# First block of a two-block transformer kernel: products in halves of the inner dimension, keys as whole fp32 products

## The reference, cut to what matters

```python
def adaln(cond, mod_w, mod_b):
    m = jax.nn.silu(cond) @ mod_w + mod_b
    return jnp.split(m, 6, axis=-1)

def modulate(x, gain, shift, scale):
    return rms_norm(x, gain) * (1 + scale) + shift

sh1, sc1, g1, sh2, sc2, g2 = [m[:, None, :] for m in adaln(c, mod_w[i], mod_b[i])]
a = modulate(h_lat, norm1_g[i], sh1, sc1)
csh1, csc1, cg1, csh2, csc2, cg2 = adaln(c_ctx, mod_w[i], mod_b[i])
ac = modulate(h_ctx, norm1_g[i], csh1, csc1)
q, k, v, p = jnp.split(h @ w_in, [ATTN_WIDTH, ATTN_WIDTH + KV_WIDTH, ATTN_WIDTH + 2 * KV_WIDTH], axis=-1)
kc, vc = jnp.split(hc @ w_in[:, ATTN_WIDTH:ATTN_WIDTH + 2 * KV_WIDTH], [KV_WIDTH], axis=-1)
```

## Time and profile before

| | |
|---|---|
| median of 3 runs | 1664.64 us (1664.16 to 1666.16) |
| profiled execution, its own time | 1665.83 us |
| its span | 1664.1 us |
| TensorE busy | 1549.9 us, 93% of the span |
| VectorE, ScalarE, GpSimd busy | 809.1, 731.3, 572.5 us |
| DMA | 327.22 MB, 197 GB/s on average |

### The profile page before, as it was taken

How to read it: one execution, slowest core, us unless ns; L and a number is a source line. 1 busy time by engine, 2 the same in 40 slices (tenths; PEclk the granted TensorE clock), 3 DMA queues, 4 the chain that set the end, 5 groups by cost and what they waited for, 6 DMA issues and landing times.

```text
span 1664.1 us, 23167 instructions
## 1 busy us (share of the span) xinstructions
PE 1549.9 (93%) x9558; PEld 1244.8 (75%) x9558; DVE 809.1 (49%) x1430; ACT 731.3 (44%) x1049; POOL 572.5 (34%) x219
## 2 busy tenths in 40 slices
PE   5999989999998999989899999999999898899997
PEld 4867867875997778568576658999886676589996
DVE  2733578423866764154744463522437633645222
ACT  3334376423436654142455344444433454354442
POOL 1300034320000442223565125655535542256543
PEclk9999889999997899999989999999999899999999
DMA  9598269769725686753344244555543333355550
GB/s 383 203 323 286 88 266 342 263 232 387 276 94 203 250 325 235 273 204 114 127 142 134 92 182 163 177 193 177 171 138 130 126 108 135 123 204 192 193 187 26
DMA packets 51225, 327.22 MB, mean 197 GB/s; under 512 B 5936, under 2 KB 5936, under 8 KB 17456
## 3 DMA queue, kind: packets, MB, share of 16 engines
q1 hardware_dynamic: 51120, 325.73, 54.6%
HBM read 324.66 MB, written 1.05 MB: 196 GB/s over the span
## 4 chain that ended last, share of the span: by engine, by line
PE 79%; DVE 13%; ACT 3%; DMA 2%; issue 1%; POOL 1%; DVEq 0%; SPq 0%; ACTq 0%
PE ps L224 20%; PE ps L225 19%; PE ps L226 19%; PE ps L221 17%; DVE lo L232 4%; DMA raw<-in_wmod 2%; PE ps L2712 1%; DVE s L240 1%; DVE pb L2763 1%; DVE s L232 1%; POOL lo L232 1%; ACT hi L229 1%; DVE pb L232 1%; DVE gl L232 1%; DVE s L2467 1%
## 5 line engine op out<-in xcount | busy, mean ns | idle before, releaser
L232 POOL TENSOR_TENSOR lo<-raw,hi 128x2048 fp32r<-128x2048 f32 (+2 forms) x76 | 350.2, 4618 | 648.1 <-ACT hi L229 648.1
L229 ACT ACTIVATE hi<-raw 128x2048 fp32r<-128x2048 f32 (+2 forms) x192 | 350.5, 1858 | 43.9 <-POOL big L232 16.9
L232 DVE TENSOR_TENSOR lo<-raw,hi 128x2048 fp32r<-128x2048 f32 (+1 forms) x116 | 298.1, 2586 | 96.4 <-ACT hi L229 96.4
L232 POOL TENSOR_TENSOR loh<-rawh,hih 128x1024 fp32r<-128x1024 f32 x56 | 137.5, 2465 | 144.4 <-ACT hih L229 144.0
L224 PE MATMUL ps<-hTh,hi 128*128 128x256 f32 x640 | 182.6, 285 | 4.9 <-DVE hTl L232 2.9
L225 PE MATMUL ps<-hTl,hi 128*128 128x256 f32 x640 | 181.6, 284 | 0.0
L226 PE MATMUL ps<-hTh,lo 128*128 128x256 f32 x640 | 181.6, 284 | 0.0
L224 PE MATMUL ps<-hi,hTh 128*128 128x512 f32 (+3 forms) x320 | 118.3, 370 | 11.6 <-DVE hTl L232 5.6
L224 PEld LDWEIGHTS ps<-hTh,hi 128*128 128x128 f32 x640 | 123.4, 193 | 6.7 <-issue 3.5
L225 PEld LDWEIGHTS ps<-hTl,hi 128*128 128x128 f32 x640 | 123.4, 193 | 0.5
L226 PEld LDWEIGHTS ps<-hTh,lo 128*128 128x128 f32 x640 | 123.3, 193 | 0.0
(11 more groups left out here) (308 smaller groups left out, 2962.1 us busy)
## 6 DMA issues: line engine op xcount, KB each, us to landing
raw<-in_wgu SPq DMA_DIRECT2D x64, 1024.0 KB, 4.9
raw<-in_wmod SPq DMA_DIRECT2D x48, 1024.0 KB, 7.1
raw<-in_wdn SPq DMA_DIRECT2D x32, 1024.0 KB, 5.6
rawh<-in_wgt SPq DMA_DIRECT2D x64, 512.0 KB, 3.9
raw<-in_wup SPq DMA_DIRECT2D x32, 1024.0 KB, 4.8
raw<-in_wdown SPq DMA_DIRECT2D x32, 1024.0 KB, 5.1
raw<-in_wz SPq DMA_DIRECT2D x12, 1024.0 KB, 4.9
raw<-in_wbr SPq DMA_DIRECT2D x8, 1024.0 KB, 4.9
```

Of the source, the lines that this page charges most:

```text
L229: return self.e.activation(o, a, f, **kw)
L232: return self.e.tensor_tensor(o, a, b, op)
```

## The change

The inner dimension is cut in two halves of 512. The modulation is taken by halves: pieces 0 and 2 (shift and scale of the lower half) first, then the lower half of both norms and the first chunk of the keys, then pieces 1 and 3 and the rest (`t_start`). ScalarE and VectorE apply scale and shift to a half (`a_half`, `v_half`). Keys and values are multiplied as whole fp32 products by `mm` (`t_keys0`), so that their chunks are not split and the context has no `yTh`, `yTl`; both row tiles of one input share a bank. q and p go by `t_half`, chunk by chunk over both row tiles. The low parts of q and p are all VectorE's, and GpSimd has no step in this block. Of `cst` the identity is loaded early and the rest later, of `col` the first 192 columns and the rest later. Small edits that the cut diff leaves out add the waits that belong to these loads.

```diff
--- before.py
+++ after.py
@@ -298,7 +299,7 @@
         l, p, i = at
         return part(t_in["wmod"][l, p], i), "raw"
     if name in ("kv", "q", "p"):
-        return part(t_in["we_" + name], at[0], 1024 if name == "kv" else PIECE), "dve" if name == "q" else "pool"
+        return part(t_in["we_" + name], at[0], 1024 if name == "kv" else PIECE), "raw" if name == "kv" else "dve"
     if name == "pm":
         return t_in["pm"], "raw"
     if name == "eo":
...
@@ -473,14 +474,16 @@
         for c in book.order:
             if c.n == 0:
                 small("sil", self.sil[:, :], self.t_in["colp"][:, 160:176])
-            elif c.n == 2:
-                small("cst", self.cst[:, :], self.t_in["cst"])
-            elif c.n == 4:
-                small("col", self.col[:, :], self.t_in["colp"])
+            elif c.key == ("mod", 0, 2, 0):
+                small("ident", self.C("ident"), self.t_in["cst"][:, 0:128])
+                small("col", self.col[:, 0:NCOL1], self.t_in["colp"][:, 0:NCOL1])
                 small("x", self.x[:, :, :], self.t_in["x"])
                 small("cx", self.cx, self.t_in["ctx"])
-            elif c.n == 10:
+            elif c.key == ("p", 0):
+                small("cst", self.cst[:, 128:NCST], self.t_in["cst"][:, 128:NCST])
                 small("row", self.row[:, :], rows(0, RKEEP))
+            elif c.key == ("pm",):
+                small("col2", self.col[:, NCOL1:NCOL], self.t_in["colp"][:, NCOL1:NCOL])
                 small("pos", self.posi[:, :], self.t_in["pos"])
                 gate(0, 0)
                 gate(0, 1)
...
@@ -690,24 +693,23 @@
...
-    def t_norm(self, t, name, src, buf):
+    def t_norm(self, t, name, src, buf, pool="B", pairs=(0, 2, 4, 6)):
         dg = self.diag(buf)
         t.wait_ge(*t.at("diag", name))
-        for k in range(0, 8, 2):
-            b = t.take("B", "norm", name, k)
+        for k in pairs:
+            b = t.take(pool, "norm", name, k)
             t.wait_ge(*t.free(b))
             for j in range(2):
                 for q in range(2):
                     m = t.mm(self.ps[:, b, 256 * j + 128 * q:256 * j + 128 * q + 128],
                              src[:, q, 128 * (k + j):128 * (k + j) + 128], dg[:, q, :], True, True)
             m.then_inc(*t.up(f"full{b}"))
-        t.mark("diag used", name)
...
@@ -982,7 +984,118 @@
         v.ts(st[:, 104:120], st[:, 56:72], 0.125, None, ALU.mult).then_inc(*v.up("dve"))
         v.mark("factors 0")
+    def sources0(self):
+        return (("a0x", self.hT, self.cadj[:, 3, :], self.mcol[:, 0:8]),
+                ("a0c", self.hTc(), self.cadj[:, 2, :], self.cadj[:, 0, :]))
+    def t_start(self, t):
+        x = self.x, self.s1
+        c = self.cx, self.s2
+        self.t_mod(t, 0, 0, "C")
+        self.t_mod_T(t, 0, 0, "C")
+        self.t_norm(t, "a0x", *x, "G", (0, 2))
+        self.t_mod(t, 0, 2, "C")
+        self.t_mod_T(t, 0, 2, "C")
+        self.t_norm(t, "a0c", *c, "M", (0, 2))
+        kv = [t.take("S", "kv", i) for i in range(2)]
+        self.t_keys0(t, kv, 0)
+        self.t_mod(t, 0, 1, "C")
+        self.t_norm(t, "a0x", *x, "G", (4, 6))
+        self.t_mod(t, 0, 3, "C")
+        self.t_mod_T(t, 0, 1, "C")
+        self.t_mod_T(t, 0, 3, "C")
+        q = [t.take("M", "q", i) for i in range(2)]
+        self.t_half(t, q, "q", 0, lambda: self.t_norm(t, "a0c", *c, "C", (4, 6)))
+        self.t_keys0(t, kv, 1)
+        self.t_half(t, q, "q", 1)
+        p = [t.take("G", "p", i) for i in range(2)]
+        self.t_half(t, p, "p", 0)
+        self.t_half(t, p, "p", 1)
+    def t_keys0(self, t, banks, i):
+        c = t.chunk("kv", i)
+        w = kn(c.raw, 4)
+        t.wait_ge(*t.at("landed", c.key))
+        for b, (name, f, *_) in zip(banks, self.sources0()):
+            if i == 0:
+                t.wait_ge(*t.free(b))
+            for q in range(2):
+                for k in range(4):
+                    if q == 0 and k % 2 == 0:
+                        t.wait_ge(*t.empty("norm", name, 4 * i + k))
+                    m = t.mm(self.ps[:, b, 256 * q:256 * q + 256], f[:, 4 * i + k, 128 * q:128 * q + 128], w[:, k, :],
+                             i == k == q == 0, i == q == 1 and k == 3)
+            if i:
+                m.then_inc(*t.up(f"full{b}"))
+        if i == 0:
+            m.then_inc(*t.up("pe"))
+        t.mark("used", c.key)
+    def t_half(self, t, banks, name, i, between=None):
+        c = t.chunk(name, i)
+        wh, wl = kn(c.hi, 4), kn(c.lo, 4)
+        t.wait_ge(*t.at("lo", c.key))
+        for q, b in enumerate(banks):
+            if i == 0:
+                t.wait_ge(*t.free(b))
+            for k in range(4):
+                t.wait_ge(*t.at("hT", "a0x", 2 * i + k // 2))
+                m = t.mm3(self.ps[:, b, :], [h[:, 4 * i + k, 128 * q:128 * q + 128] for h in self.H3],
+                          (wh[:, k, :], wl[:, k, :]), i == k == 0, i == 1 and k == 3)
+            if i:
+                m.then_inc(*t.up(f"full{b}"))
+            if q == 0 and between is not None:
+                between()
+        if i == 0:
+            m.then_inc(*t.up("pe"))
+        t.mark("used", c.key)
+    def a_half(self, a, i):
+        a.wait_ge(*a.at("scale 0", i))
+        for name, f, scale, shift in self.sources0():
+            b = a.bank("norm", name, 4 * i + 2)
+            a.wait_ge(*a.full("norm", name, 4 * i + 2))
+            for k in (4 * i + 2, 4 * i + 3):
+                j = k % 2
+                m = a.ac(f[:, k, :], self.ps[:, b, 256 * j:256 * j + 256], ACT.Identity, scale=scale[:, k:k + 1],
+                         bias=shift[:, k:k + 1])
+            m.then_inc(*a.up(f"free{b}"))
+        for k in (4 * i, 4 * i + 2):
+            a.wait_ge(*a.empty("norm", "a0x", k))
+            a.ac(self.H3[0][:, k:k + 2, :], self.hT[:, k:k + 2, :]).then_inc(*a.up("act"))
+            a.mark("hT hi", "a0x", k)
+    def v_half(self, v, i):
+        n = slice(4 * i, 4 * i + 4)
+        gain = self.K("n1a", 4 * i, 4)
+        for j in range(2):
+            v.wait_ge(*v.at("mcol", 0, j, i))
+        v.stt(self.cadj[:, 3, n], self.mcol[:, 8 + 4 * i:12 + 4 * i], 1.0, gain, ALU.add, ALU.mult)
+        v.stt(self.cadj[:, 2, n], self.cadj[:, 1, n], 1.0, gain, ALU.add, ALU.mult).then_inc(*v.up("dve"))
+        v.mark("scale 0", i)
+        v.wait_ge(*v.last)
+        for name, f, scale, shift in self.sources0():
+            b = v.bank("norm", name, 4 * i)
+            v.wait_ge(*v.full("norm", name, 4 * i))
+            for k in (4 * i, 4 * i + 1):
+                j = k % 2
+                m = v.ts(f[:, k, :], self.ps[:, b, 256 * j:256 * j + 256], scale[:, k:k + 1], shift[:, k:k + 1],
+                         ALU.mult, ALU.add)
+            m.then_inc(*v.up(f"free{b}"))
+        for k in (4 * i, 4 * i + 2):
+            v.wait_ge(*v.at("hT hi", "a0x", k))
+            v.tt(self.H3[1][:, k:k + 2, :], self.hT[:, k:k + 2, :], self.H3[0][:, k:k + 2, :].bitcast(F32),
+                 ALU.subtract).then_inc(*v.up("dve"))
+            v.mark("hT", "a0x", k // 2)
     def t_qk(self, t):
+        t.wait_ge(*t.at("in", "cst"))
         for i in (5, 4, 0, 1, 2, 3):
             b = t.take("B", "qk", i)
             c0 = 128 * i if i < 5 else 1280
...
@@ -3238,17 +3354,7 @@
     def tensor(self, t):
         H, Y = self.H3, self.Y3
-        for p in range(4):
-            self.t_mod(t, 0, p)
-            if p:
-                self.t_mod_T(t, 0, p - 1)
-        self.t_mod_T(t, 0, 3)
-        self.t_norm(t, "a0x", self.x, self.s1)
-        self.t_norm(t, "a0c", self.cx, self.s2)
-        both = [(H, ("hT", "a0x"), 0), (H, ("hT", "a0x"), 1)]
-        self.t_rows(t, ("kv",), ("kv",), 256, both + [(Y, ("hT", "a0c"), 0), (Y, ("hT", "a0c"), 1)])
-        self.t_rows(t, ("q",), ("q",), 512, both)
-        self.t_rows(t, ("p",), ("p",), 512, both)
+        self.t_start(t)
         t.book.enter()
         self.t_qk(t)
         self.t_heads0(t)
...
@@ -3278,15 +3384,17 @@
     def scalar(self, a):
         H, Y = self.H3, self.Y3
         self.a_silu(a)
+        self.a_mod(a, 0, 0)
         self.a_stats(a, "a0x", self.x, lambda h, t: a.at("in", "x"), self.s1, 0, ("sil",))
         self.a_stats(a, "a0c", self.cx, lambda h, t: a.at("in", "cx"), self.s2, 32)
-        for p in range(4):
-            self.a_mod(a, 0, p)
-        self.a_split(a, "kv", 0, ahead=1)
-        self.a_norm(a, "a0x", self.cadj[:, 3, :], self.mcol[:, 0:8], self.hT, H, [("scale", 0, 0)], [])
-        self.a_norm(a, "a0c", self.cadj[:, 2, :], self.cadj[:, 0, :], self.hTc(), Y, [("scale c",)], [])
-        self.a_split(a, "kv", 1)
-        self.a_split(a, "q", 1)
+        self.a_mod(a, 0, 2)
+        self.a_half(a, 0)
+        self.a_split(a, "q", 0, ahead=0)
+        self.a_mod(a, 0, 1)
+        self.a_mod(a, 0, 3)
+        self.a_split(a, "q", 1, ahead=0)
+        self.a_half(a, 1)
+        self.a_split(a, "p", 1, ahead=0)
         self.a_queries0(a)
         for t in range(2):
             b = a.bank("p", t)
...
```

(35 more changed lines are left out.)

12 lines of the change are left out of this document (8 added, 4 removed).

## The result

| | before, median us (runs) | changed, median us (runs) | ratio, 95% interval |
|---|---|---|---|
| first comparison | 1665.40 (4) | 1653.78 (4) | 0.9937 [0.9914, 0.9960] |
| second | 1665.62 (16) | 1654.10 (6) | 0.9941 [0.9925, 0.9956] |
| third | 1666.31 (22) | 1655.20 (6) | 0.9943 [0.9925, 0.9961] |

The change is faster by 11.1 to 11.6 us, 0.6%. The forecast was faster by 4.7 us (1659.9), with a range down to 1657.2: the sign was right, the size was not. The profiled execution of the changed kernel took 1656.71 us with a span of 1654.9; two more profiles of it have spans of 1651.3 and 1649.9. Three executions that took far longer than the others of their kernel (1775 us and more) are left out of the ratios and of every mean.

What follows compares the result with a forecast made beforehand. The first 78 us were taken as 35 us of DMA supply, then 43 us of TensorE products; p's end 4.8 us earlier, less 0.1 at the hand-over, gave 4.7 off 1664.64: 1659.9 us, range 1657.2 to 1663.6.

Steps and rivals of the forecast that it cites:

- x's landing: Loads at the start: 3.34 MB fewer ahead of x, so x lands at 12.6 us instead of 21.15.
- The pieces in the upper half: TensorE, modulation pieces 1 and 3 after the first half of the keys: 2.3 us each.
- Whole products: TensorE, keys and values: 32 whole fp32 products at 0.46 us, 14.8 us against 11.6 for 96 split ones.
- The hand-over: From p's end to the pooled products: second transpose waits for ScalarE's copy of p, 0.1 us taken, 0.6 at most.
- What lies beside: VectorE, ScalarE and GpSimd beside TensorE: low parts hidden, keys ready at 65.1, queries at 70.4, 2.7 us before wanted.
- the low parts' move gains nothing by itself: Opening: taking p's low parts off GpSimd gains nothing alone, since those 7 us were hidden before.
- The low clock: Rival, TensorE in the opening: slow rate lasts through the keys' first half, 10.0 us more, 1669.9 us; chance 0.07.
- VectorE's queue: Rival, ahead of q's transposes: p's last chunk 5 us later, TensorE waits 2.3 us, 1662.2 us; chance 0.09.
- Small transfers: Rival, loads ahead of x: two small loads hold the queue, x lands 3.6 us later, 1663.5 us; chance 0.06.
- What ends the block earlier moves all that follows by as much: Everything behind the opening: shifts by the opening's gain, its own length unchanged.
- The bound of 7.4 us for the gain: Fast end of the range: all TensorE steps fast from the start and x at 12.0 us, giving 1657.2 us.

Runs made afterwards that it cites:

- the repetition: The changed kernel run again with nothing altered, against the kernel before: 1654.10 us, ratio 0.9941.
- the twelve products: Changed kernel plus twelve unread 128x128 identity products on TensorE ahead of the norm of x, against the kernel before: 1654.52 us, ratio 0.9937.

## Why the prediction was wrong, step by step

**The opening, by the prediction's own steps**, with the profile shown first (us, from one start to the next):

| step | predicted | measured | earlier by |
|---|---|---|---|
| start of the norm of x | 17.75 | 17.05 | 0.70 |
| norm of x, lower half | 3.4 | 3.70 | -0.30 |
| piece 2, eviction, transpose | 3.7 | 3.58 | 0.12 |
| norm of the context, lower half | 1.9 | 1.95 | -0.05 |
| keys, first half | 7.4 | 7.08 | 0.32 |
| piece 1, norm, piece 3, transposes | 7.6 | 6.32 | 1.28 |
| q, first half, with the context's norm | 7.4 | 7.35 | 0.05 |
| keys, second half | 7.4 | 6.71 | 0.69 |
| q, second half, and p | 16.5 | 16.53 | -0.03 |

Together 2.8 us: 73.1 was forecast for p's end, and it is 70.27. The mechanism of the opening was right, and no step is out of place. Mis-sized were mainly three terms, all three too long.

- *x's landing.* 12.6 was taken as the middle of 13.2 and 12.0; it is 11.84. The count forwards from the first chunk was the nearer one.
- *The pieces in the upper half.* 2.3 each came from two groups of 32 records, 1.23 and 1.08, the first of them right behind a slow group. 64 records in one go take 1.95, and the next group starts 1.88 to 1.89 behind.
- *Whole products.* 0.46 us was the busy time of a group of eight, which holds the tail of its last product. From one group's start to the next it is 3.26 to 3.55 for eight, 0.43 each: 13.8 us for 32, and 2.2 over the 11.6 of the split ones instead of 3.2. The Trainium skill's page "FP8 and Floating Point Precision", section TensorE Precision Notes, gives four passes to true fp32; by four for three the estimate was 15.5, and the measured ratio is 1.19, not 1.33, so here the measurement decides.

**The hand-over** cost 0.36 (2.68 us from p's end to the pooled products instead of 2.32), not 0.1: the wait of 0.47 for the copy of p is there as named. The two other profiles are 0.9 us ahead because of piece 2, which the prediction put between its slow and fast rate.

**What lies beside** held in its times. VectorE ended the last low part at 53.96 (forecast 56.5), since ScalarE had rounded both chunks of q before it came to p's; the second half of the keys ends at 53.74 and the copies start at 54.35, so they were hidden with nothing to spare. The keys were ready at 62.49 (65.1), the queries at 67.76 (70.4), 2.5 us before they were wanted (2.7). That the low parts' move gains nothing by itself was wrong in both orders: in the new one it is worth about 0.9 us of the opening, since with GpSimd's low parts the queries are ready at 71.42, behind p's end at 69.61; in the old one it costs 3.7 us, since the copies stand behind the low parts.

**The rivals.** The low clock came, but only in the lower half of the norm (0.50), where the forecast's 3.4 us had it priced in, and in one of three profiles in piece 2; the keys ran fast. VectorE's queue did not make TensorE wait. Small transfers cost nothing that shows: x landed even before the forward count.

**"What ends the block earlier moves all that follows by as much"** is the step that took the time out of the range. It holds to the hundredth for the next 59.82 us. Further on, the mean of the changed kernel's rest is 2.8 us shorter than that of before, 1580.4 against 1583.2, in work that the change doesn't touch. With the opening's gain alone, 7.3 to 8.2 us, the medians of before would come down to 1657.2 to 1659.0, inside the range. The bound of 7.4 us for the gain was a bound for the opening, which one profile kept (7.3) and two broke (8.2), by the three terms above, and nothing was added for a rest that differs by several us from one execution to the next; 1664.1 of span came from one execution. That the mean moved, and not only single executions, is measured; why is open.

## What to carry to other kernels

Take the price of a product from one group's start to the next start, not from the busy time of a short group: the tail of the last product lies under the work that follows. Bytes ahead of the first operand were worth here what they take at the full DMA rate (3.02 us for 1.24 MB), until the next load in the order (here q's weights) is the bound; and low-part work is free only as long as its queue ends ahead of the copies that free the banks. For a change of half a percent, compare the stretch that was changed in the profiles, and take from the total no more than its scatter behind that stretch allows.

## What the runs showed of the hardware that was not expected

- The granted clock column of the first profile reads 1.00 while the norm of x runs at half speed (3.78 us for 16 records, 2.05 later). In the repetition the same 3.78 us stand at 0.50, and with the twelve products at 0.54. The Trainium skill's page "TensorE: Matmul & The Clock Gate", Part 1, Seeing it yourself, warns that the recorded clock events are not reliable; these runs agree, and the duration of a known group is the better witness.
- Waits of 1.75 and 1.77 us ahead of the same key products were followed by a granted clock of 1.00 in two executions of the kernel before, and a wait of 1.76 by 0.61 and 0.53 in one execution of it with p's low parts on VectorE.
- Three tables of 128x128 on VectorE, 0.56 us of work, cost 9.30 us beside a GpSimd split of 10.13: the price was set by the other engine's instructions, not by those that met them.
